# Expert stage: result stores on ScalarE's queue, and a landing tile with a GpSimd copy for the gathered rows

## The chip, the core and the metric

The kernel runs on one core of a Trainium2 chip. Its time is the device time of one execution, in microseconds; lower is better. TensorE multiplies, VectorE, ScalarE and GpSimd work on tiles, SyncE only issues DMAs. All five engines run their own instruction streams and wait for each other on semaphores.

## What is computed

The reference is a transformer block with attention, gated linear attention and a mixture of experts, followed by a second block. Only the mixture of experts matters here. 512 tokens choose 4 of 32 experts each. Cut to the core:

```python
top_v, top_i = lax.top_k(logits, TOP_K)                 # T=512 tokens, TOP_K=4, N_EXPERTS=32
gates = jax.nn.softmax(top_v, axis=-1)
...
def expert_block(args):
    idx, e = args
    xb = xpad[idx]                                      # the rows of this expert's tokens
    gu = xb @ w_gate_up[e] + b_gate_up[e]               # 1024 -> 2 x 1024
    x_glu = jnp.minimum(gu[:, ::2], SWIGLU_LIMIT)
    x_lin = jnp.clip(gu[:, 1::2], -SWIGLU_LIMIT, SWIGLU_LIMIT)
    act = x_glu * jax.nn.sigmoid(SWIGLU_ALPHA * x_glu) * (x_lin + 1.0)
    return act @ w_down[e] + b_down[e]                  # 1024 -> 1024
```

Everything is float32. Each expert has 12 MB of weights. The rows are then weighted with the gates and summed per token, which is done in a later stage.

## The kernel before

The expert stage is `stage_experts`, line 1536 on. Tokens are grouped by expert into units of 32 slots. An expert has as many units as its tokens need, at least one, so the number of units is known only at run time; each engine reads it from a table and loops over the units (`Fori(1, units)`), with the first unit written out ahead of the loop.

A row of 1024 numbers is laid out as four quarters of 256: the 128 partitions of the tile `rows` are 4 quarters x 32 slots. For a unit, TensorE does the following, in this order: the up part (L1727: eight slabs, each times a piece of the transposed rows), the down part of the unit before (L1750: four slabs), the transposes of the hidden values (L1736), the transposes of the rows of the next unit but one (`turn_rows`, L1704), and the bias (L1714).

Weights come as slabs of 1 MB, twelve per expert (8 up, 4 down). SyncE loads them in order, once per expert (L1653), into 18 slots of `staging`; a slot is free when the last unit of its expert has used it (`free`, L1627 on), and SyncE waits for the slab loaded four before (`arrived`, L1637). A quarter of each slab is used where it lies. The other three quarters are copied into a `ring` of four places, by VectorE (L1853, eight slabs of a unit) or ScalarE (L1785, four).

The rows of a unit come by an indirect DMA that GpSimd issues. `gather(i)` reads the unit's code from the table, waits until the last gather has landed and until TensorE has transposed the rows that lie in `rows` (semaphore `rows_ps`), copies the slot numbers (L1673), and issues the DMA (L1676) into `rows`. Gather 0 goes into the tile `y`, which is not in use yet.

The result of a unit is read from PSUM into the one tile `y` by ScalarE (`read_y`, L1808), which waits for the semaphore `y_free`. `store_rows` on GpSimd waits for that read, issues the store to `expert_rows` in HBM (L1683), waits until it has landed, and gives `y` back. The order on GpSimd inside the loop is

```python
with pool.Fori(1, units) as i:
    gather(i + 2)
    store_rows(i)
```

so the next gather is issued behind the landing of the store. The last result is stored by SyncE (L1660). On ScalarE the order in the loop is: ring copies, `gate` (L1791), `rows_turned` (L1802), a ring copy, `read_y`, `hidden_turned` (L1796).

Of the kernel before, what the change touches and what calls it, by code (L numbers as in the profile page):

```python
# [21 lines left out]
P = 128  # L22
S = 512
NT = S // P
D = 1024
# [7 lines left out]
NE, TOPK = 32, 4  # L33
# [1502 lines left out]
def stage_experts(k):  # L1536

    nc, d = k.nc, k.d
    with ExitStack() as ctx:
# [5 lines left out]
        quarter = sb("quarter", [P, P])  # L1545
        pick = sb("pick", [P, P], F32R)
        slot = sb("slot", [P, LINE], I32)
        rows = sb("rows", [P, D // QUARTERS])
        rowsT = sb("rowsT", [P, 2, P])
        lin = sb("lin", [P, GLU])  # L1550
# [14 lines left out]
        slot_ready = sem("slot_ready")  # L1565
        slot_seen = sem("slot_seen")
        rows_in = sem("rows_in")
        rows_ps = sem("rows_ps")
        rowsT_ready = sem("rowsT_ready")
        chunk_in = sem("chunk_in")  # L1570
# [6 lines left out]
        turned_ps = sem("hidden_turned_ps")  # L1577
        hT_ready = sem("hiddenT_ready")
        y_read = sem("expert_y_read")
        y_out = sem("expert_y_out")  # L1580
        y_free = sem("expert_y_free")
        last_out = sem("expert_last_out")
        settled = sem("early_settled")
        gate_diff = sem("gate_diff")
        gate_exp = sem("gate_exp")
# [32 lines left out]
        def store_of(n):  # L1618
            return d["expert_rows"][bass.ds(n, SLOTS), :].rearrange("r (c n) -> c r n", c=QUARTERS)

        with nc.Block() as block:
            @block.sync
            def _(sp):
                up = lambda e, q: d["w_gate_up"][(e * KT + q) * P:(e * KT + q + 1) * P, :]
                down = lambda e, m: d["w_down"][(e * 4 + m) * P:(e * 4 + m + 1) * P, :]

                def free(c, last):  # L1627

                    if c < KT:
                        sp.wait_ge(chunk_done, last * CHUNKS + (c + 1))  # L1630
                    else:
                        sp.wait_ge(chunk_done, last * CHUNKS + (CHUNKS + c + 1))

                def arrived(m):

                    sp.wait_ge(raw_in[m % STAGED], 16 * (m // STAGED + 1))
                    sp.sem_inc(chunk_in, 1)  # L1637

                for c in range(QUARTERS):
                    sp.dma_start(raw_bias[c * NE:(c + 1) * NE, :], d["b_gate_up"][:, c * PART:(c + 1) * PART]  # L1640
                                 ).then_inc(bias_in, 16)
                sp.dma_start(quarter[:], d["quarters"]).then_inc(quarter_in, 16)
                for m in range(EARLY - AHEAD):
                    arrived(m)
                for m in range(EARLY, NE * CHUNKS):
                    e, c = m // CHUNKS, m % CHUNKS
                    old = m - STAGED
                    if old >= 0:
                        if old % CHUNKS == 0 or old == 0:
                            of = old // CHUNKS  # L1650
                            last = sp.value_load(k.table[0:1, ENDS + of:ENDS + of + 1], min_val=0, max_val=NBLK - 1)
                        free(old % CHUNKS, last)
                    sp.dma_start(staging[:, m % STAGED * CHUNK:(m % STAGED + 1) * CHUNK],  # L1653
                                 up(e, c) if c < KT else down(e, c - KT)).then_inc(raw_in[m % STAGED], 16)
                    arrived(m - AHEAD)
                for m in range(NE * CHUNKS - AHEAD, NE * CHUNKS):
                    arrived(m)
                end = sp.value_load(k.table[0:1, TABLE - 2:TABLE - 1], min_val=NE - 1, max_val=NBLK - 1)
                sp.wait_ge(y_read, end + 1)
                sp.dma_start(store_of(end * SLOTS), y[:]).then_inc(last_out, 16)  # L1660
                sp.wait_ge(last_out, 16)

            @block.gpsimd
            def _(pool):
                units = units_on(pool)
                by_quarter = d["h2"].rearrange("t (c n) -> (t c) n", c=QUARTERS)

                def gather(i, out=rows, at=0):
                    code = pool.value_load(k.table[0:1, bass.ds(i + P, 1)], min_val=0, max_val=CODES - 1)
                    if out is rows:  # L1670
                        after(pool, rows_in, 16 * i)
                        after(pool, rows_ps, i)
                    pool.tensor_copy(slot[:, at:at + 1], k.slots[:, bass.ds(code, 1)]).then_inc(slot_ready, 1)  # L1673
                    pool.wait_ge(slot_ready, i + 1)
                    pool.sem_inc(slot_seen, 1)
                    pool.indirect_dma_start(  # L1676
                        out=out[:], out_offset=None, in_=by_quarter,
                        in_offset=bass.IndirectOffsetOnAxis(ap=slot[:, at:at + 1], axis=0)).then_inc(rows_in, 16)

                def store_rows(n):  # L1680

                    pool.wait_ge(y_read, n)
                    pool.dma_start(store_of(n * SLOTS - SLOTS), y[:]).then_inc(y_out, 16)  # L1683
                    pool.wait_ge(y_out, 16 * n)
                    pool.sem_inc(y_free, 1)

                gather(0, y, 1)
                gather(1)
                gather(2)
                with pool.Fori(1, units) as i:  # L1690
                    gather(i + 2)
                    store_rows(i)
                pool.wait_ge(rows_in, 16 * units + 32)

            @block.tensor
            def _(pe):
# [1 line left out]
                ident = k.sq[:, IDENT, :]  # L1698

                def turn_rows(i, src=rows):  # L1700
                    pe.wait_ge(rows_in, 16 * i + 16)
                    after(pe, rowsT_ready, i)
                    for b in range(2):
                        mm = pe.transpose(k.bank(6)[:, b * P:(b + 1) * P], src[:, b * P:(b + 1) * P], ident)  # L1704
                    mm.then_inc(rows_ps, 1)
# [73 lines left out]
            def _(act):  # L1779
# [24 lines left out]

                def read_y(n, done):
                    act.wait_ge(chunk_done, done)
                    act.wait_ge(y_free, n + 1)
                    act.activation(y[:], k.bank(4)[:, 0:GLU], ACT.Copy).then_inc(y_read, 1)  # L1808

                act.sem_inc(y_free, 1)  # L1810
                rows_turned(0, 0)
                fill(0, 0, 2)
                act.wait_ge(bias_set, 1)
# [13 lines left out]
                with act.Fori(1, units) as i:  # L1827
                    e = expert_on(act, i)
                    fill(i, e, 5)
                    fill(i, e, 7)  # L1830
                    fill(i, expert_on(act, i - 1), 10)
                    gate(i)
                    rows_turned(i + 1, i * CHUNKS + KT)
                    fill(i + 1, expert_on(act, i + 1), 2)
                    read_y(i - 1, i * CHUNKS + CHUNKS)
                    hidden_turned(i)
                act.wait_ge(act_filled, units * len(BY_ACT) + 1)
                act.sem_inc(act_filled, 2)
# [2 lines left out]
                act.activation(k.gates[:], k.gates[:], ACT.Exp).then_inc(gate_exp, 1)  # L1841
                end = act.value_load(k.table[0:1, TABLE - 2:TABLE - 1], min_val=NE - 1, max_val=NBLK - 1)
                read_y(end, units * CHUNKS + CHUNKS)

            @block.vector
            def _(dve):
# [1273 lines left out]
```

## Time and profile before

| | |
|---|---|
| Median of 3 runs | 2101.05 us (2095.19 to 2104.95) |
| The profiled execution | 2098.68 us |
| Its span in the profile | 2097.1 us |
| TensorE busy | 1704.3 us, 81% |
| VectorE busy | 1136.5 us |
| ScalarE busy | 853.6 us |
| GpSimd busy | 257.8 us |
| Mean granted TensorE clock | 0.897 of full speed |
| DMA | 516.46 MB, mean 246 GB/s |

The profile is one execution. The page of the profile lists each engine's busy time, the span in 40 slices, and the costliest groups of instructions; the trace behind it gives single instructions with their start, the idle time of their engine ahead of them and what ended it. The expert stage is the stretch from about 376 to 1694 us. A granted clock of 1.00 is 2.4 GHz, 0.50 is 1.2 GHz.

### The profile page before, as it was taken

The numbers are of one execution on the slowest core, as the hardware profiler recorded it, in microseconds if no ns is written. First come the engines' busy times: TensorE is split into PE (matmuls) and PEld (weight loads), VectorE is DVE, ScalarE is ACT, GpSimd is POOL, SyncE is SP. The second block draws the span as 40 slices with busy tenths as digits, with TensorE's granted clock in tenths as the row PEclk, the third lists the DMA queues.
The fourth block names the chain that finished last, engine by engine and source line by source line (L and its number), as shares of the span: only waits on it lengthen the run. The fifth ranks groups of instructions, "written<-read, shape, count | busy, mean of one in ns | idle before, by whom it ended". The sixth has DMA issues, their size and how long they took to land. (4 is left out here: it accounts for less than half of the span.)

```text
span 2097.1 us, 50062 instructions
## 1 busy us (share of the span) xinstructions
PE 1704.3 (81%) x16925; PEld 894.4 (43%) x16926; DVE 1136.5 (54%) x1698; ACT 853.6 (41%) x1131; POOL 257.8 (12%) x304
## 2 busy tenths in 40 slices
PE   6999898677977787878887787879778657999797
PEld 4999644232332332323332233323323125777763
DVE  5874536554654554545654555546545356694555
ACT  5344521543543443434543444434444234442421
POOL 0000000211111111111111111111111030151000
PEclk9999998897998888989987889889988777999999
DMA  8871840659478866995389985997598983231011
GB/s 301 277 242 33 216 190 21 260 220 423 163 305 335 336 265 259 394 381 221 137 343 404 424 337 222 371 400 302 205 415 344 417 308 80 73 91 42 4 52 40
DMA packets 135287, 516.46 MB, mean 246 GB/s; under 512 B 19927, under 2 KB 58728, under 8 KB 85929
## 3 DMA queue, kind: packets, MB, share of 16 engines
q1 hardware_dynamic: 117016, 483.74, 58.9%
q0 software_dynamic: 18048, 31.20, 4.5%
q8 instruction: 51, 0.84, 0.2%
q10 hardware_dynamic: 146, 0.48, 0.1%
q14 instruction: 26, 0.21, 0.0%
HBM read 492.44 MB, written 22.81 MB: 246 GB/s over the span
## 5 line engine op out<-in xcount | busy, mean ns | idle before, releaser
L1853 DVE COPY ring<-staging 128x1536 f32 (+1 forms) x638 | 600.5, 967 | 578.0 <-PE banks L1727 464.3
L1785 ACT ACTIVATE ring<-staging 128x1536 f32 (+1 forms) x319 | 473.8, 1487 | 731.6 <-PE banks L1727 545.9
L1727 PE MATMUL banks<-staging,rowsT 128*32 (+1 forms) x1268 | 633.5, 654 | 42.4 <-DVE ring L1853 21.3
L1727 PE MATMUL banks<-ring,rowsT 128*32 128x512 f32 x3840 | 641.9, 655 | 0.0
L1727 PEld LDWEIGHTS banks<-staging,rowsT 128*32 128x32 f32 x1268 | 140.8, 118 | 480.8 <-issue 476.6
L1750 PE MATMUL banks<-staging,hiddenT 128*32 x1280 | 294.0, 383 | 1.6 <-DVE ring L1853 1.3
L1750 PE MATMUL banks<-ring,hiddenT 128*32 128x256 f32 x3840 | 294.8, 383 | 0.0
L1704 PE MATMUL banks<-sq,rows 128*128 128x128 f32 x162 | 41.1, 343 | 234.5 <-DMA rows<-h_rows,slot 234.5
L1750 PEld LDWEIGHTS banks<-staging,hiddenT 128*32 128x32 f32 x1280 | 141.7, 111 | 153.7 <-issue 47.3
L1750 PEld LDWEIGHTS banks<-ring,hiddenT 128*32 128x32 f32 x3840 | 155.3, 111 | 0.0
L1727 PEld LDWEIGHTS banks<-ring,rowsT 128*32 128x32 f32 x3840 | 155.2, 118 | 0.0
L602 PE MATMUL banks<-w_in_hi,hT 128*128 128x256 f32 (+1 forms) x768 | 147.3, 291 | 1.5 <-issue 1.5
L1673 POOL COPY slot<-slots 128x1 int32 x82 | 30.2, 368 | 878.5 <-issue 857.8
L2196 PE MATMUL banks<-h3T,w_in_hi 128*128 128x512 f32 x400 | 129.4, 405 | 1.4 <-DVE h3T L2374 1.4
L1704 PEld LDWEIGHTS banks<-sq,rows 128*128 128x128 f32 x162 | 21.0, 165 | 245.1 <-DMA rows<-h_rows,slot 245.1
L602 PEld LDWEIGHTS banks<-w_in_hi,hT 128*128 128x128 f32 x768 | 122.5, 194 | 3.5 <-issue 3.5
L1683 POOL DMA_DIRECT2D expert_rows<-y_rows x79 | 62.8, 795 | 388.6 <-ACT y_rows L1808 365.7
L602 PE MATMUL banks<-w_in_lo,hT 128*128 128x256 f32 (+1 forms) x384 | 109.7, 286 | 0.0
L1676 POOL DMA_INDIRECT rows<-h_rows,slot x81 | 96.4, 1190 | 66.6 <-POOL slot L1673 51.0
L2196 PEld LDWEIGHTS banks<-h3T,w_in_hi 128*128 128x128 f32 x400 | 76.1, 191 | 23.1 <-issue 4.1
L2196 PE MATMUL banks<-h3T,w_in_lo 128*128 128x512 f32 x200 | 78.9, 395 | 0.0
L602 PEld LDWEIGHTS banks<-w_in_lo,hT 128*128 128x128 f32 x384 | 74.5, 194 | 1.9 <-issue 1.9
(434 smaller groups left out, 1939.2 us busy)
## 6 DMA issues: line engine op xcount, KB each, us to landing
staging<-in_w_gate_up SPq DMA_DIRECT2D x250, 1024.0 KB, 11.5
staging<-in_w_down SPq DMA_DIRECT2D x128, 1024.0 KB, 12.8
stage<-in_w_mod SPq DMA_DIRECT2D x21, 1024.0 KB, 5.8
stage<-in_w_in SPq DMA_DIRECT2D x25, 512.0 KB, 4.0
stage<-in_w_in SPq DMA_DIRECT2D x11, 1024.0 KB, 6.1
expert_rows<-y_rows POOLq DMA_DIRECT2D x79, 128.0 KB, 8.6
expert_rows<-catT SPq DMA_DIRECT2D x1, 7936.0 KB
early<-in_w_gate_up SPq DMA_DIRECT2D x6, 1024.0 KB, 12.9
```

What stands on the lines that cost most here:

```text
L602: mm = pe.matmul(k.bank(4 + t)[:, 0:w], hT[:, a, q, tt], b[:, q, :], start=(q == 0 and a == 0 and b is hi), stop=(q == KT - 1 and a == 1))
L1673: pool.tensor_copy(slot[:, at:at + 1], k.slots[:, bass.ds(code, 1)]).then_inc(slot_ready, 1)
L1676: pool.indirect_dma_start(out=out[:], out_offset=None, in_=by_quarter, in_offset=bass.IndirectOffsetOnAxis(ap=slot[:, at:at + 1], axis=0)) ...
L1683: pool.dma_start(store_of(n * SLOTS - SLOTS), y[:]).then_inc(y_out, 16)
L1704: mm = pe.transpose(k.bank(6)[:, b * P:(b + 1) * P], src[:, b * P:(b + 1) * P], ident)
L1727: mm = pe.matmul(k.bank(0)[c * SLOTS:(c + 1) * SLOTS, :], rowsT[:, q % 2, row], w, start=first and q == 0, stop=not first and q == KT - 1, ...
L1750: mm = pe.matmul(k.bank(4)[c * SLOTS:(c + 1) * SLOTS, 0:GLU], hT[:, b, m * SLOTS:(m + 1) * SLOTS], w, start=(m == 0 and b == 0), stop=(m = ...
L1785: act.activation(ring[:, pos % RING, :], staged(i, e, pos, PART, CHUNK - PART), ACT.Copy).then_inc(act_filled, 1)
L1853: dve.tensor_copy(ring[:, pos % RING, :], staged(i, e, pos, PART, CHUNK - PART)).then_inc(dve_filled, 1)
L2196: mm = pe.matmul(k.bank(n % 4), w[:, n % NW, q, :], hT[:, b, q, :], start=(q == 0 and a == 0), stop=(q == KT - 1 and a == 2))
```

## The change

- The result rows are stored by ScalarE's DMA queue: `store_y` follows `read_y` on ScalarE, and waits for ScalarE's own copy. `read_y` waits for the landing of the store before (semaphore `y_out`); `y_free` and `last_out` are gone, as is SyncE's final store.
- A new tile `landing`, as large as `rows`. From the third on, all gathers go into it. GpSimd copies `landing` to `rows` (`move_rows`) when TensorE has transposed what lay in `rows`, and then issues the next gather. So the loop on GpSimd is `move_rows(i + 2)`, `gather(i + 3)`. The first three gathers go to three tiles and wait for nothing of each other.
- TensorE's `turn_rows` waits for the semaphore `rows_here`, that the GpSimd copy sets, in place of the gather's own.

```diff
@@ SyncE
-                end = sp.value_load(k.table[0:1, TABLE - 2:TABLE - 1], min_val=NE - 1, max_val=NBLK - 1)
-                sp.wait_ge(y_read, end + 1)
-                sp.dma_start(store_of(end * SLOTS), y[:]).then_inc(last_out, 16)
-                sp.wait_ge(last_out, 16)
@@ GpSimd
-                def gather(i, out=rows, at=0):
+                def gather(i, out, at, done):
                     code = pool.value_load(k.table[0:1, bass.ds(i + P, 1)], min_val=0, max_val=CODES - 1)
-                    if out is rows:
-                        after(pool, rows_in, 16 * i)
-                        after(pool, rows_ps, i)
                     pool.tensor_copy(slot[:, at:at + 1], k.slots[:, bass.ds(code, 1)]).then_inc(slot_ready, 1)
...
-                def store_rows(n):
-
-                    pool.wait_ge(y_read, n)
-                    pool.dma_start(store_of(n * SLOTS - SLOTS), y[:]).then_inc(y_out, 16)
-                    pool.wait_ge(y_out, 16 * n)
-                    pool.sem_inc(y_free, 1)
-
-                gather(0, y, 1)
-                gather(1)
-                gather(2)
+                def move_rows(i):
+                    pool.wait_ge(rows_in, 16 * i - 16)
+                    pool.wait_ge(rows_ps, i)
+                    pool.sem_inc(rows_free, 1)
+                    pool.tensor_copy(rows[:], landing[:]).then_inc(rows_here, 1)
+                    pool.wait_ge(rows_here, i + 1)
+                    pool.sem_inc(rows_moved, 1)
+
+                gather(0, y, 1, first_in[0])
+                gather(1, rows, 2, first_in[1])
+                gather(2, landing, 0, rows_in)
+                for m in range(2):
+                    pool.wait_ge(first_in[m], 16)
+                    pool.sem_inc(rows_here, 1)
+                move_rows(2)
+                gather(3, landing, 0, rows_in)
                 with pool.Fori(1, units) as i:
-                    gather(i + 2)
-                    store_rows(i)
-                pool.wait_ge(rows_in, 16 * units + 32)
+                    move_rows(i + 2)
+                    gather(i + 3, landing, 0, rows_in)
+                pool.wait_ge(rows_in, 16 * units + 16)
@@ TensorE
                 def turn_rows(i, src=rows):
-                    pe.wait_ge(rows_in, 16 * i + 16)
+                    pe.wait_ge(rows_here, i + 1)
@@ ScalarE
                 def read_y(n, done):
                     act.wait_ge(chunk_done, done)
-                    act.wait_ge(y_free, n + 1)
+                    act.wait_ge(y_out, 16 * n + 16)
                     act.activation(y[:], k.bank(4)[:, 0:GLU], ACT.Copy).then_inc(y_read, 1)
 
-                act.sem_inc(y_free, 1)
+                def store_y(n):
+                    act.wait_ge(y_read, n + 1)
+                    act.sem_inc(y_seen, 1)
+                    act.dma_start(store_of(n * SLOTS), y[:]).then_inc(y_out, 16)
+
+                act.sem_inc(y_out, 16)
...
                     read_y(i - 1, i * CHUNKS + CHUNKS)
+                    store_y(i - 1)
                     hidden_turned(i)
...
                 read_y(end, units * CHUNKS + CHUNKS)
+                store_y(end)
+                act.wait_ge(y_out, 16 * units + 16)
+                act.sem_inc(y_seen, 1)
```

## Rows read from the trace of the kernel before

**Rows 1.** TensorE's waits, 370 to 1700 us: in total, times, longest (us).
```profile
PE banks L1704 <- DMA rows<-h_rows,slot: 234.5, 41, 9.6
PE banks L1727 <- DVE ring L1853: 21.3, 18, 6.0
PE banks L1727 <- ACT ring L1785: 14.1, 11, 1.9
```

**Rows 2.** Timeline of TensorE's L1704 and GpSimd: start, us, what, [idle before <-releaser].
```profile
914.17 0.38 PE L1704 MATMUL banks<-sq,rows 128*128 128x128 f32 x2
933.77 0.69 PE L1704 MATMUL banks<-sq,rows 128*128 128x128 f32 x2 [7.78 <-DMA rows<-h_rows,slot]
948.37 0.38 PE L1704 MATMUL banks<-sq,rows 128*128 128x128 f32 x2
...
915.86 0.76 POOL L1683 DMA_DIRECT2D expert_rows<-y_rows  x1 [9.28 <-ACT y_rows L1808]
925.60 0.75 POOL L1673 COPY slot<-slots 128x1 int32 x1 [8.98 <-issue]
927.18 0.99 POOL L1676 DMA_INDIRECT rows<-h_rows,slot  x1 [0.82 <-ACT y_rows L1808]
```

**Rows 3.** Issue to landing by line: first the stores L1683, then the gathers L1676.
```profile
DMA to landing us min/median/max: 3.7/8.6/9.9
...
DMA to landing us min/median/max: 2.7/6.1/7.9
```

**Rows 4.** Timeline of TensorE's L1704 where no weights are being loaded.
```profile
1005.03 0.38 PE L1704 MATMUL banks<-sq,rows 128*128 128x128 f32 x2
...
1029.35 0.38 PE L1704 MATMUL banks<-sq,rows 128*128 128x128 f32 x2
```

**Rows 5.** Stretches: PE, PEld, DVE, ACT, POOL busy, PEclk, DMA share, GB/s.
```profile
1005.00:1029.00 24.00, 23.00 (x268) 9.37 (x266) 16.51 (x23) 13.76 (x17) 5.06 (x6) 1.00 0.08 22
1140.00:1180.00 40.00, 28.25 (x256) 9.88 (x256) 16.96 (x22) 14.15 (x17) 4.90 (x7) 0.73 1.01 424
484.00:492.00 8.00, 6.85 (x78) 2.91 (x75) 3.63 (x6) 3.92 (x5) 1.09 (x2) 0.66 1.01 427
```

**Rows 6.** SyncE's waits for free slots, 370 to 1700 us: total, times, longest.
```profile
SPq L1653 <- PE banks L1727: 420.5, 104, 68.7
...
SPq L1653 <- PE banks L1750: 250.2, 107, 16.1
```

**Rows 7.** Issue to landing of the weight slabs, L1653, 370 to 1700 us.
```profile
DMA to landing us min/median/max: 4.7/12.1/15.1
```

**Rows 8.** Timeline of TensorE in a unit of an expert with one unit.
```profile
482.19 1.06 PE L1727 MATMUL banks<-staging,rowsT 128*32 x1 [1.14 <-DVE ring L1853]
...
485.28 1.05 PE L1727 MATMUL banks<-staging,rowsT 128*32 x1 [1.15 <-ACT ring L1785]
```

**Rows 9.** Timeline of ScalarE, behind a result read and at the kernel's start.
```profile
949.25 0.38 ACT L1796 ACTIVATE hiddenT<-banks 128x256 f32<-128x256 f32 x1
951.36 1.49 ACT L1785 ACTIVATE ring<-staging 128x1536 f32 x1 [1.73 <-PE banks L1727]
...
0.92 0.41 ACTq L422 DMA_DIRECT2D sq<-in_square  x1
```

**Rows 10.** First and last turn of the loop, and L1808: min/median/max ns, first and last start.
```profile
395.50 0.38 PE L1704 MATMUL banks<-sq,rows 128*128 128x128 f32 x2
...
1687.54 0.44 PE L1704 MATMUL banks<-sq,rows 128*128 128x128 f32 x2 [0.41 <-DMA rows<-h_rows,slot]
...
L1808 ACT ACTIVATE y_rows<-banks x80: 362/366/384, 409.9 to 1693.7; 128x256 f32<-128x256 f32 x80
```

**Rows 11.** A GpSimd copy (busy, mean ns), all ring copies L1853, and one of them.
```profile
L2320 POOL COPY sums<-z 128x512 f32<-128x512 f32 x4 | 2.9, 719 | 104.3 <-ACT z L2258 104.1
...
L1853 DVE COPY ring<-staging x638: 940/960/1196, 387.4 to 1690.7; 128x1536 f32 x158, 128x1536 f32<-128x1536 f32 x2
...
950.46 1.12 DVE L1853 COPY ring<-staging 128x1536 f32 x1 [0.69 <-PE banks L1727]
```

More of the change, by code:

```diff
@@ L1547, in stage_experts @@
         slot = sb("slot", [P, LINE], I32)
+        landing = sb("rows_landing", [P, D // QUARTERS])
         rows = sb("rows", [P, D // QUARTERS])
@@ L1567, in stage_experts @@
         rows_in = sem("rows_in")
+        first_in = [sem(f"first_rows{m}_in") for m in range(2)]
+        rows_here = sem("rows_here")
+        rows_free = sem("rows_free")
+        rows_moved = sem("rows_moved")
         rows_ps = sem("rows_ps")
@@ L1579, in stage_experts @@
         y_read = sem("expert_y_read")
+        y_seen = sem("expert_y_seen")
         y_out = sem("expert_y_out")
-        y_free = sem("expert_y_free")
-        last_out = sem("expert_last_out")
         settled = sem("early_settled")
@@ L1677, in gather @@
                         out=out[:], out_offset=None, in_=by_quarter,
-                        in_offset=bass.IndirectOffsetOnAxis(ap=slot[:, at:at + 1], axis=0)).then_inc(rows_in, 16)
-                def store_rows(n):
-                    pool.wait_ge(y_read, n)
-                    pool.dma_start(store_of(n * SLOTS - SLOTS), y[:]).then_inc(y_out, 16)
-                    pool.wait_ge(y_out, 16 * n)
-                    pool.sem_inc(y_free, 1)
-                gather(0, y, 1)
-                gather(1)
-                gather(2)
+                        in_offset=bass.IndirectOffsetOnAxis(ap=slot[:, at:at + 1], axis=0)).then_inc(done, 16)
+                def move_rows(i):
[13 more added lines that the diff above has]
+                gather(3, landing, 0, rows_in)
                 with pool.Fori(1, units) as i:
-                    gather(i + 2)
-                    store_rows(i)
-                pool.wait_ge(rows_in, 16 * units + 32)
+                    move_rows(i + 2)
+                    gather(i + 3, landing, 0, rows_in)
+                pool.wait_ge(rows_in, 16 * units + 16)
             @block.tensor
```

## Prediction, made before the change was run

> **What bounds the kernel now.** I read the page first for where TensorE is busy, then TensorE's waits in the expert stage, then the stretch of one unit on TensorE and GpSimd, then SyncE's waits and the DMA rates, because a wait that goes will show what is behind it. The loop of the expert stage, 79 units on TensorE, runs from the row transposes at 395.5 us to those at 1687.5 us [rows 10], so 1292 of 2097 us; the last result is read at 1693.7. In the stage TensorE waits for almost one thing: 234.5 us, in 41 waits, for the gathered rows in front of the transposes of L1704, against 21.3 and 14.1 us for weight copies into the ring [rows 1]. The weights are not late today because this wait gives them time.
>
> The wait comes from one tile and one queue. GpSimd issues the store of unit n's result, waits until it has landed, and only then copies the next slot numbers and issues the next gather. In the stretch of [rows 2] TensorE turned rows at 914.17, the store went out at 915.86, the slot copy ran at 925.60, the gather was issued at 927.18, and TensorE went on at 933.77 after 7.78 us idle: 17.9 us from store to rows. Store and gather take a median of 8.6 and 6.1 us to land [rows 3]. The next turn, at 948.37, was 14.6 us later without a wait. So a pair costs 948.37 - 914.17 = 34.2 us, 17.1 us per unit. Where no weights are on the way (22 GB/s), two units take 1029.35 - 1005.03 = 24.3 us [rows 4, 5]: 12.1 us per unit, at a granted clock of 1.00. The average of the loop is 1292 / 79 = 16.35.
>
> **What the change removes.** It takes the 8-us store landing off GpSimd and gives the gather a tile of its own. After turn n on TensorE, GpSimd copies rows n+1 over and issues the gather n+2: copy with its waits under 2 us, slot copy to issue 1.6 us (925.60 to 927.18, [rows 2]), landing at most 7.9 us [rows 3]: about 11.5 us after the turn. Those rows are needed by the second turn after, at least 24 us on. So I take the rows wait to zero: 234.5 us, and 2.5 us of the first gathers, which no longer wait for each other. After each such wait TensorE also ran slow: turn to turn it took 14.6 us here, against 12.1. Over the loop this is what is left: 1292 - 79 x 12.1 - 234.5 - 36 = 66 us. If nothing else came late, the loop would be 79 x 12.1 = 956 us.
>
> **What is late next: the weights.** This is the term that decides. Each expert's weights are loaded once, 12 slabs of 1.049 MB, however many units of 32 slots it has. With the DMA engines saturated the traffic is 424 GB/s at a share of 1.01 [rows 5], so a slab takes 2.47 us, an expert's twelve 29.6 us, and the gather and store of one unit (262 KB) 0.6 us. An expert with n units gives TensorE 12.1 n us of work. So n = 1 falls 18.1 us short, n = 2 falls 6.6 us short, n = 3 gains 4.9. SyncE says the same of today's schedule: it waits 420.5 + 250.2 = 671 us for free slots, up to 68.7 us at once [rows 6]. The loading is idle behind long experts and cannot be ahead by more than the ring of 18 slots.
>
> How many units each expert has follows from the reference's router on its own inputs: 5 1 2 5 3 2 2 3 3 3 2 2 2 7 2 2 1 2 2 3 4 2 2 2 3 4 1 2 3 1 1 1, 80 in all, as many as L1808 has instructions [rows 10]. The lead behind a long expert I work out so. I take it that at the start of its last unit the ring holds the next expert's first six slabs. The first slot is free 0.9 us later, the first slab lands 4.7 us after its issue (shortest landing, [rows 7]), one more takes 2.5, its ring copy 1.1: 9.2 us. TensorE comes to the last up-slab of the expert behind it after 12.1 + 6.0 us. The difference less 0.6 us of the unit's own traffic is 8.3 us. Then run by run: experts 1-2: 18.1 + 6.6 - 8.3 = 16.4; 5-6: 4.9; 10-12: 11.5; 14-18: 36.2; 21-23: 11.5; 26-27: 16.4; 29-30, with only the 4.9 gained by expert 28 before them: 31.3. Sum 128 us of waiting for weights, against 36 today. Such a unit is to be seen now: from 482.19 to 485.28 us one slab's matmuls follow the other's at 3.1 us, with a wait of 1.15 us for the ring before each [rows 8], and in 484 to 492 the granted clock is 0.66 [rows 5]. TensorE's next four slabs, already there, then ran at the lower level for some 2.5 us, 1.3 us dearer. Seven runs to all 15 waiting units: 9 to 20, I take 12.
>
> **What it adds.** ScalarE: behind each result read it now waits for its own copy (0.37 us), then issues a DMA. Its DMA issue at the kernel's start took 0.41 us [rows 9]; with address arithmetic I allow 0.7 us. That pushes hiddenT (949.25) by 0.7 us, which TensorE needs 7 us later, behind the whole up part, and the next ring copy at 951.36 has 1.73 us of idle in front of it [rows 9]. Cost nothing; if that cover were gone, 0.7 x 80 = 56 us. GpSimd: one copy of 128x256 per unit. No such copy is in the trace; one of 128x512 took 719 ns [rows 11], so between 0.36 and 0.72; I take 0.5. On GpSimd itself it is free. Against VectorE it may cost: a ring copy that began at 950.46, while GpSimd issued its store, took 1.12 us instead of 0.96 [rows 11]. That store issue leaves GpSimd, the copy comes. Bounds: from a gain of 79 x 0.16 = 13 us to a loss of 79 x 0.5 = 40 us if each copy stood before a ring copy that TensorE waits for. Most ring copies have over 1 us of slack, so 5. ScalarE's read of the next result now waits for its queue's own store; it has 11 us for the 8.6 of today's [rows 3]: nothing, and rival (d) otherwise. The final store, SyncE's so far, is one DMA from another queue: nothing.
>
> The Trainium skill, on its page "SBUF — State Buffer", section "Who interferes with whom", speaks against this part: VectorE in its two-port copy mode and GpSimd share a port pair as an exclusive lock, and whichever comes second blocks for the whole instruction. The 1.12 us row agrees in kind, as a partial overlap would. By that rule alone the term would be the 40 us just named.
>
> **The sum.** The turn that closes unit 0 is at 395.5 now [rows 10] and 2.5 us earlier then: 393.0. 79 units x 12.1 = 955.9. Weights 128. Restart at the slow clock 12. Lock 5. That gives 1494 for the last turn, at 1687.5 now [rows 10]. The last expert's four down-slabs come some 3 us late: 1497. So the gain is 190 us. The profiled execution took 2098.7 us, so 1908.7; the median of the runs shown is 2.4 us above it, 2101.05, so 1911.
>
> **The rivals.**
> (a) The lock decides: the GpSimd copy delays a ring copy on TensorE's path in most units. For it: the 1.12 us row, and the copy comes right at the unit's edge, when VectorE fills the next unit's first slabs. Against it: VectorE's ring copies have a maximum of 1.20 us over 638 today, though GpSimd works beside them. 35 us more: 1946.
> (b) The lead is worth nothing, since gathers and stores also break into the slab stream: seven runs x 8.3 us = 58 us more: 1969.
> (c) The lead is worth more, a whole six slabs (15 us): five runs save 6.5 us, and run 5-6 the 4.9: some 37 us less: 1874.
> (d) The other side: ScalarE's store lands behind the slabs. SyncE's slabs take 12.1 us to land in the median and 15.1 at most [rows 7]. ScalarE's next read waits for its last store, so a unit can't be shorter than the landing and 0.9 us. Below 11 us this is free, and the idle 1.73 us of ScalarE take it to some 13; at the slabs' 15.1 in every unit the loop is 79 x 16 = 1264 us, 2073, and from 15.5 on (16.35 - 0.9) the change is slower than before: 17 us would give 79 x 17.9 = 1414 us, 2223. Against it: GpSimd's store landed in 8.6 us among the same slabs.
> (e) It doesn't do what it says: a copy or a semaphore in GpSimd's chain keeps rows late. The chain of 11.5 us would have to double. Then 2100.
>
> **How the numbers follow.** My forecast, with its terms off by up to 20 us either way, 0.62: 1890 to 1931. (a) 0.12, (b) 0.09, (c) 0.08, (d) 0.06, of which 0.03 slower than before and the rest between 2000 and 2090, (e) 0.03. The range reaches to (c) and (b), 1872 to 1972; outside lie (d), (e) and tails. 0.5% is 10 us, about what a measurement of this kernel can tell from no change. Faster: all but (e) and a half of (d): 0.94. Same 0.03, slower 0.03.
>
> **What would show it.** TensorE's waits at L1704 for the gathered rows, 234.5 us, should be under 10, and no wait for the GpSimd copy should stand in their place. TensorE's waits for VectorE's and ScalarE's ring copies should rise from 36 to between 90 and 150 us, in the units of the runs named, above all the last three experts and experts 14 to 18. Units elsewhere should repeat at 12.1 us. The DMA rate over the loop should rise by a sixth (1292 / 1101). ScalarE's store should land in under 12 us. VectorE's ring copies should stay near 0.97 us in the mean; 1.1 or more would be (a). I am wrong if rows waits remain, or if weight waits sum to over 200 us.

## The result: half the forecast gain

| | before | changed |
|---|---|---|
| Median | 2098.12 us (4 runs) | 1999.86 us (4 runs, 1998.11 to 2001.35) |
| Ratio | | 0.9528, 95% interval 0.9499 to 0.9556 |
| Profiled execution | 2098.68 us | 1999.55 us |
| Span | 2097.1 us | 1997.8 us |
| Loop of 79 units, first to last turn of rows | 395.5 to 1687.5: 1292 us | 395.9 to 1589.5: 1194 us |

The change is 98 us faster, where 190 was forecast; the time lies above the range of 1872 to 1972. All of the difference is in the loop. The last row is from the timeline of TensorE, where these two lines are the turns that [rows 10] has for before:

```profile
395.85 0.63 PE L1707 MATMUL banks<-sq,rows 128*128 128x128 f32 x2
...
1589.54 0.38 PE L1707 MATMUL banks<-sq,rows 128*128 128x128 f32 x2
```

The view of waits, 370 to 1600 us, says what TensorE waits for now (total, times, longest), and the last line what ScalarE does:

```profile
PE banks L1730 <- ACT ring L1788: 149.8, 92, 4.7
PE banks L1730 <- DVE ring L1865: 33.6, 32, 5.4
...
ACT y_rows L1811 <- DMA expert_rows<-y_rows: 97.5, 36, 4.5
```

The wait for rows in L1704, 234.5 us in [rows 1], is gone altogether: L1707 has none left but that for the very first gather. The new wait is for ring copies, as forecast, but nearly all of it for ScalarE's (14.1 us before), and ScalarE itself waits 97.5 us for its own stores. That is the wait that rival (d) named. ScalarE's timeline in one unit (start, us, what, idle before and its releaser) shows its size:

```profile
900.60 0.39 ACT L1811 ACTIVATE y_rows<-banks 128x256 f32<-128x256 f32 x1 [1.63 <-DMA expert_rows<-y_rows]
901.25 1.07 ACTq L1816 DMA_DIRECT2D expert_rows<-y_rows  x1
902.42 0.38 ACT L1799 ACTIVATE hiddenT<-banks 128x256 f32<-128x256 f32 x1 [1.44 <-PE banks L1730]
903.85 2.86 ACT L1788 ACTIVATE ring<-staging 128x1536 f32 x2 [1.04 <-PE banks L1730]
...
916.62 0.38 ACT L1811 ACTIVATE y_rows<-banks 128x256 f32<-128x256 f32 x1 [4.01 <-DMA expert_rows<-y_rows]
```

The store is issued at 901.25, and the next read starts at 916.62, after 4.01 us of waiting for it: 15.4 us of landing, where GpSimd's stores had a median of 8.6 and a maximum of 9.9 [rows 3]. The issue holds ScalarE for 1.07 us (0.41 in [rows 9]), and hiddenT comes 1.82 us after the start of the read; before, the two started 0.26 us apart.

### The profile page after: what moved, and what is told of

Same layout as the page of the kernel before. It is cut to its first block and busy times, and to the rows that moved or that the text cites. A ratio compares the mean times of both kernels' runs of the same rounds, so it can differ in the third digit from the quotient of the medians.

```text
span 1997.8 us, 50227 instructions
## 1 busy us (share of the span) xinstructions
PE 1695.5 (85%) x16925; PEld 877.7 (44%) x16926; DVE 1139.1 (57%) x1698; ACT 859.4 (43%) x1131; POOL 326.4 (16%) x307
## 5 line engine op out<-in xcount | busy, mean ns | idle before, releaser
L1730 PE MATMUL banks<-staging,rowsT 128*32 (+1 forms) x1268 | 650.1, 654 | 185.0 <-ACT ring L1788 149.8
L1730 PE MATMUL banks<-ring,rowsT 128*32 128x512 f32 x3840 | 661.1, 656 | 0.0
L1730 PEld LDWEIGHTS banks<-staging,rowsT 128*32 128x32 f32 x1268 | 128.8, 115 | 630.3 <-issue 625.4
L1681 POOL COPY rows<-rows_landing 128x256 f32<-128x256 f32 x80 | 74.8, 935 | 794.9 <-PE banks L1707 794.9
L1730 PEld LDWEIGHTS banks<-ring,rowsT 128*32 128x32 f32 x3840 | 144.9, 115 | 0.0
L1673 POOL DMA_INDIRECT rows_landing<-h_rows,slot x81 | 133.4, 1647 | 64.3 <-POOL slot L1670 64.3
L1670 POOL COPY slot<-slots 128x1 int32 x83 | 49.4, 595 | 276.0 <-issue 206.2
L1874 DVE TENSOR_SCALAR lin<-banks 128x256 f32<-128x256 f32 x80 | 34.0, 425 | 96.3 <-PE banks L1730 96.3
L1799 ACT ACTIVATE hiddenT<-banks 128x256 f32<-128x256 f32 x80 | 30.7, 384 | 113.0 <-PE banks L1730 98.7
L1811 ACT ACTIVATE y_rows<-banks 128x256 f32<-128x256 f32 x80 | 30.0, 375 | 108.3 <-DMA expert_rows<-y_rows 97.5
## 6 DMA issues: line engine op xcount, KB each, us to landing
staging<-in_w_gate_up SPq DMA_DIRECT2D x250, 1024.0 KB, 13.3
staging<-in_w_down SPq DMA_DIRECT2D x128, 1024.0 KB, 13.3
```

The lines of the kernel that those rows point to most:

```text
L1673: pool.indirect_dma_start(out=out[:], out_offset=None, in_=by_quarter, in_offset=bass.IndirectOffsetOnAxis(ap=slot[:, at:at + 1], axis=0)) ...
L1681: pool.tensor_copy(rows[:], landing[:]).then_inc(rows_here, 1)
L1730: mm = pe.matmul(k.bank(0)[c * SLOTS:(c + 1) * SLOTS, :], rowsT[:, q % 2, row], w, start=first and q == 0, stop=not first and q == KT - 1, ...
L1799: act.activation(hT[:].rearrange("p b n -> p (b n)"), k.bank(2)[:, 0:2 * P], ACT.Copy, scale=1.0 / ALPHA).then_inc(hT_ready, 1)
L1874: dve.tensor_scalar(lin[:], k.bank(0)[:, GLU:PART], LIMIT + 1.0, 1.0 - LIMIT, ALU.min, ALU.max).then_inc(lin_ready, 1)
```

## Experiments

The theories: **A**, ScalarE waits for the landing of its own store; **B**, the issue of the store on ScalarE makes its ring copies late; **C**, the GpSimd copy locks VectorE out; **D**, the weights are later than the ledger has them (the ledger is the prediction's count of slab time against unit time, expert by expert); later **E**, ScalarE's stores slow the weights. All loops below are from the first to the last turn of rows of the profiled execution, as above. The diffs are cut to the lines that matter.

| Kernel | median, us | ratio to before | loop, us |
|---|---|---|---|
| changed | 1999.9 | 0.953 (0.950 to 0.956) | 1194 |
| ScalarE's stores, no landing wait | 1948.8 | 0.931 (0.928 to 0.934) | 1141 |
| the same, issue moved | 1932.8 | 0.923 (0.914 to 0.932) | 1130 |
| the same, no stores in the loop | | | 1069 |
| GpSimd's stores, landing tile | 1902.9 | 0.909 (0.9065 to 0.9114) | 1096 |
| GpSimd's stores, wait moved only | 1933.2 | 0.923 (0.9211 to 0.9250) | 1127 |
| ScalarE's stores only | 1991.7 | 0.951 (0.948 to 0.955) | 1182 |

A ratio is to the kernel before in the same set of runs; in the five sets that kernel's medians lie between 2089.7 and 2098.1 us, so a few microseconds between two rows' medians mean nothing. A loop is of one execution; for two versions that differ only in GpSimd's copies it is 1095.8 and 1095.9. The versions without the landing wait, with the issue moved and with no stores in the loop leave the results out: what they store is an unchanged tile. The last stores it behind the loop, in one execution, so only its loop is compared.

### Take ScalarE's wait for the landing away

The result is read into another tile, so that no DMA has to have landed; the stores go on, without the results.

```diff
                 def read_y(n, done):
                     act.wait_ge(chunk_done, done)
-                    act.wait_ge(y_out, 16 * n + 16)
-                    act.activation(y[:], k.bank(4)[:, 0:GLU], ACT.Copy).then_inc(y_read, 1)
+                    act.activation(y_kept[:], k.bank(4)[:, 0:GLU], ACT.Copy).then_inc(y_read, 1)
```

> The changed kernel, with ScalarE reading each result into a tile of its own that no DMA touches, so that no result read waits for the landing of the store before. ScalarE still issues all 80 stores, which now send an unchanged tile: the stored rows are not the results. Theory A (landing: the store on ScalarE's queue lands about 15 us after its issue while slabs are on the way, against 8.6 from GpSimd; ScalarE waits for it and its ring copies come late): the loop falls from 1193 to 1100-1115 us, the time to 1908-1925, TensorE's waits for ScalarE's ring copies from 150 to 60 us or less. Theory B (issue: the 1.07 us that ScalarE spends on issuing a store, and the 1.4 us in front of hiddenT, use up its slack): stays at 1985-2000. Theory C (the GpSimd copy locks VectorE out) and theory D (weights are later than the ledger has them): stays at 1985-2000.

Measured: 1948.8 us, loop 1141, against 1908 to 1925 and 1100 to 1115 expected. A is true, and it is worth 51 us (53 of loop), not the 85 it was to explain. TensorE still waits 79.9 us for ScalarE's ring copies, 102 times, and 52.5 us for VectorE's:

```profile
PE banks L1731 <- ACT ring L1789: 79.9, 102, 2.3
PE banks L1731 <- DVE ring L1865: 52.5, 44, 4.4
```

### Give the stores back to GpSimd, keep the rest

```diff
                 with pool.Fori(1, units) as i:
                     move_rows(i + 2)
                     gather(i + 3, landing, 0, rows_in)
+                    pool.wait_ge(y_read, i)
+                    pool.sem_inc(y_seen, 1)
+                    pool.dma_start(store_of(i * SLOTS - SLOTS), y[:]).then_inc(y_out, 16)
...
                     read_y(i - 1, i * CHUNKS + CHUNKS)
-                    store_y(i - 1)
```

ScalarE still waits for `y_out` ahead of a read; GpSimd issues and goes on.

> The changed kernel, with the stores issued by GpSimd again, behind the gather in its loop, but without GpSimd waiting for their landing: ScalarE waits for it, as in the changed kernel. Landing tile and GpSimd copy stay. Theory A: the store lands in 8.6 us as in the kernel before, no wait of ScalarE is left, and the time is the one predicted for the change, 1905-1925. Theory B: the issue leaves ScalarE too, the same. Theories C and D: 1985-2000, since copy and weights are as in the changed kernel.

Measured: 1902.9 us (1897.3 to 1904.1), ratio 0.909. Of the versions that do all the work this is the fastest (a variant of it, below, is equal), 97 us faster than the changed kernel, and it is where the forecast put the change (1911). Copy and landing tile are in it, so C and D don't hold in that size. The lines are the turns that bound the loop and, between them, three turns in a row: 11.51 us for a unit with nothing late, then 22.24 us for one that waits for weights:

```profile
391.96 0.38 PE L1715 MATMUL banks<-sq,rows 128*128 128x128 f32 x2
...
1191.86 0.38 PE L1715 MATMUL banks<-sq,rows 128*128 128x128 f32 x2
1203.37 0.38 PE L1715 MATMUL banks<-sq,rows 128*128 128x128 f32 x2
1225.61 0.38 PE L1715 MATMUL banks<-sq,rows 128*128 128x128 f32 x2
...
1487.74 0.38 PE L1715 MATMUL banks<-sq,rows 128*128 128x128 f32 x2
```

### Fewer slabs under way

SyncE waits for the slab loaded two before, in place of four before.

```diff
-AHEAD = 4
+AHEAD = 2
```

> The changed kernel with SyncE waiting for the slab loaded two before instead of four before, so that about three slabs instead of five are under way when ScalarE issues a store. Theory A, with the store queued behind the slabs: it lands some 5 us sooner (10 us), ScalarE's waits for it (97 us) nearly go, and the time falls to 1915-1950 unless three slabs under way load more slowly. Theories B and C: no change, 1995-2005. Theory D: slower if anything.

Measured: 2005.7 us, ratio to before 0.958 (0.954 to 0.961), no gain over the changed kernel. The slabs' own landing fell from a median of 13.3 to 8.0 us (first line; the view of L1657), but the store's did not (the other two, ScalarE's timeline): issued at 843.95, still waited for until 858.53, 14.6 us.

```profile
DMA to landing us min/median/max: 4.7/8.0/10.1
...
843.95 1.07 ACTq L1816 DMA_DIRECT2D expert_rows<-y_rows  x1
858.53 0.38 ACT L1811 ACTIVATE y_rows<-banks 128x256 f32<-128x256 f32 x1 [1.51 <-DMA expert_rows<-y_rows]
```

So the picture in rival (d), a store queued behind the slabs, is wrong. What is left of it is the number.

### Halve the slabs' packets

Each slab is loaded by two DMAs of half its columns, so that a run in a partition is 4 KB.

```diff
-                    sp.dma_start(staging[:, m % STAGED * CHUNK:(m % STAGED + 1) * CHUNK],
-                                 up(e, c) if c < KT else down(e, c - KT)).then_inc(raw_in[m % STAGED], 16)
+                    for part in range(2):
+                        at, size = m % STAGED * CHUNK, CHUNK // 2
+                        sp.dma_start(staging[:, at + part * size:at + (part + 1) * size],
+                                     (up(e, c) if c < KT else down(e, c - KT))[:, part * size:(part + 1) * size]
+                                     ).then_inc(raw_in[m % STAGED], 16)
```

> The changed kernel, each 1 MB slab loaded by two DMAs of half its columns, so that a partition's run is 4 KB instead of 8 KB and the slabs' packets are half as long. In the changed kernel the packets of ScalarE's store are served from 3.9 to 14.3 us after its issue, and the same with two slabs fewer under way, so it doesn't wait behind the slabs but takes turns with them. If turns are taken packet by packet (A1), halved slab packets bring the store's last packet to 8-10 us, ScalarE's waits of 97 us for it nearly go, and the time falls to 1945-1965. If it is ScalarE's own issue of 1 KB rows that is slow (A2), the landing and the time stay: 1995-2005.

Measured: 1976.9 us, ratio to before 0.945 (0.943 to 0.947), the loop 1174: some 20 us faster than the changed kernel, where one theory had 35 or more and the other nothing. The mechanism of the first is there. The DMA view counts the packets of ScalarE's queue (q10; packets, MB, share). In the changed kernel, of the store issued at 901.25, 72 of its 132 packets are served in the first ten microseconds (901.3 to 911.3) and 60 after them (911.3 to 917):

```profile
q10 hardware_dynamic: 72, 0.07, 2.1%
...
q10 hardware_dynamic: 60, 0.06, 2.9%
```

With halved slab packets, of the store issued at 889.76, 128 in the first ten (889.7 to 899.7):

```profile
q10 hardware_dynamic: 128, 0.13, 3.7%
```

ScalarE's wait for its stores is gone. The store's 1 KB packets take turns with the slabs' packets, so what sets its landing is how long one turn of the other lasts, not how much of the other is queued. The Trainium skill, page "DMA: Bandwidth & Descriptors", section "Queues, rings and completion order", has it that a DMA engine goes round its queues packet by packet. The trace agrees: at the end of the store of 901.25, from 911.8 to 915.6, slab and store packets come in nearly equal numbers.

```profile
q1 hardware_dynamic: 45, 0.34, 20.9%
q10 hardware_dynamic: 48, 0.05, 3.6%
```

The shares say more: together 24.5% of 16 engines, so four are at work, and all of the store that is left is on them. Turns with 8 KB packets explain the 11 us only if the whole store is on these four, 32 packets on each: a slab packet takes 0.309 us in the trace and one of the store 0.046, and 32 turns of both are 11.4 us. From its first to its last packet the store took 11.1 us (905.2 to 916.3). The same sum holds in the other cases: with packets of 4 KB (0.159 us) 6.6 us, measured 6.3; with two slabs fewer under way 11.4 again, measured 10.8; where no slabs flow 1.5, measured 1.7.

For the weights halved packets are no gain (two take 0.318 us, one of 8 KB 0.309), and their waits at the ring stay, 85.7 and 65.3 us; for that part the expectation had too much.

### Move ScalarE's issue to where it is idle

In the version without the landing wait, the store's issue goes behind the pair of ring copies with which ScalarE's next turn of the loop begins. [rows 9] had 1.73 us of idle time behind hiddenT; that was the cover of this cost.

```diff
                     fill(i, e, 5)
                     fill(i, e, 7)
+                    act.dma_start(store_of(i * SLOTS - SLOTS), y[:]).then_inc(y_out, 16)
                     fill(i, expert_on(act, i - 1), 10)
...
                     read_y(i - 1, i * CHUNKS + CHUNKS)
-                    store_y(i - 1)
                     hidden_turned(i)
```

> The version without the landing wait (1949 us; it stores an unchanged tile), with ScalarE's store issue moved from behind the result read to behind the second ring copy of the next unit, where ScalarE waits about 1.1 us for TensorE anyway. Theory B (what is left of the loss, 1949 against 1903, is the place of the 1.07 us issue: it makes the ring copy of slab 5 0.4 us late in every unit): TensorE's tenth step of the up part starts 0.43 us after the one before instead of 0.8, a unit with nothing late takes 11.5 us instead of 11.9, and the time falls to 1903-1925. If the issue costs ScalarE this wherever it stands, or the rest is the store's own traffic on ScalarE's queue, it stays at 1940-1955.

Measured: 1932.8 us, 16 us faster (the intervals of the two ratios just meet), the loop 11 us shorter, and a unit with nothing late takes 11.51 us instead of 11.91, as B says. Where the 0.4 us sits is to be seen on TensorE in the changed kernel, at the tenth step of the up part, slab 5, which ScalarE copies; the pair of copies above it starts at 933.47:

```profile
933.47 2.86 ACT L1788 ACTIVATE ring<-staging 128x1536 f32 x2 [1.05 <-PE banks L1730]
...
934.30 0.59 PE L1730 MATMUL banks<-staging,rowsT 128*32 x1
935.10 0.61 PE L1730 MATMUL banks<-staging,rowsT 128*32 x1 [0.19 <-ACT ring L1788]
935.55 0.59 PE L1730 MATMUL banks<-staging,rowsT 128*32 x1
```

and in the version with GpSimd's stores, in the same unit, the steps follow at 0.43 us without a break, and ScalarE's two copies stand apart:

```profile
879.91 1.49 ACT L1796 ACTIVATE ring<-staging 128x1536 f32 x1 [1.74 <-PE banks L1738]
881.56 1.49 ACT L1796 ACTIVATE ring<-staging 128x1536 f32 x1 [0.16 <-PE banks L1738]
...
881.59 0.59 PE L1738 MATMUL banks<-staging,rowsT 128*32 x1
882.02 0.59 PE L1738 MATMUL banks<-staging,rowsT 128*32 x1
```

The time missed its expectation of 1903 to 1925. 58 units became 0.4 us shorter, 23 us, but the units that wait for weights got longer. 34 us of loop remain against the version with GpSimd's stores, all of them in such units (unit 31: 21.4 against 14.1 us).

### No stores in the loop at all

The version with the issue moved, its stores taken out of the loop and sent by SyncE behind the last slab.

```diff
+                sp.wait_ge(first_in[0], 16)
+                for n in range(NBLK):
+                    sp.dma_start(store_of(n * SLOTS), y[:]).then_inc(y_out, 16)
+                sp.wait_ge(y_out, 16 * NBLK)
...
-                    act.dma_start(store_of(i * SLOTS - SLOTS), y[:]).then_inc(y_out, 16)
...
-                store_y(end)
```

> The version with the store issue moved, now with no store in the loop at all; SyncE writes all 94 blocks of 32 rows from an unchanged tile behind the last slab instead, so only the loop (first to last turn of rows) is to be compared, not the time. With ScalarE's stores in it the loop takes 1130 us, with GpSimd's 1096. In the first, slabs land 13.4 us after their issue in the median, in the second 12.5. Theory E (stores on ScalarE's queue slow the stream of slabs, by more than their bytes): slabs land in 12.0-12.5 us and the loop takes 1075-1096 us. If the 34 us between the two have another cause on ScalarE or VectorE, only the stores' 10.5 MB go, at 424 GB/s 25 us less a part that is hidden: 1110-1130 us.

Measured: loop 1069 us, under the range of E (1075 to 1096). So the same 80 stores, of the same bytes, cost 1096 - 1069 = 27 us of loop from GpSimd's queue, and 1130 - 1069 = 61 us from ScalarE's. This run takes ScalarE's issue out of the loop together with the traffic, and the loop alone can't tell them apart; the stream of slabs can. Its landing is slower with ScalarE's stores than with none and with GpSimd's, in this order (in the first, the landing of only 60 or so slabs is known):

```profile
DMA to landing us min/median/max: 6.4/13.5/14.9
...
DMA to landing us min/median/max: 4.7/12.4/14.7
...
DMA to landing us min/median/max: 4.8/12.5/15.5
```

In seven stretches, 217 slabs in all, SyncE issues slab after slab, under 4 us apart, in all three versions. These take 540.3 us with no stores, 553.9 with GpSimd's (38 of them fall in) and 591.8 with ScalarE's (36). A store costs the slabs 0.36 us from GpSimd and 1.43 us from ScalarE, and the 38 us between the two are all of the 34 that are asked for. In the longest of the stretches, 60 slabs and ten stores, the columns are those of [rows 5]; again ScalarE's stores, none, GpSimd's:

```profile
954.20:1117.84 163.64, 130.37 (x1262) 43.47 (x1258) 79.75 (x105) 66.90 (x76) 22.88 (x30) 0.86 1.01 411
...
928.62:1078.60 149.98, 124.89 (x1256) 44.86 (x1260) 79.31 (x104) 66.87 (x77) 28.76 (x30) 0.90 1.01 427
...
935.83:1089.06 153.23, 124.97 (x1237) 44.21 (x1233) 78.66 (x103) 64.11 (x73) 31.12 (x38) 0.89 1.01 425
```

What sets the two queues apart is to be seen where no slabs flow. The DMA view of one store alone, ScalarE's in the changed kernel (930.9 to 935) and then GpSimd's (878.7 to 883.5):

```profile
DMA packets 132, 0.13 MB, mean 32 GB/s; under 512 B 4, under 2 KB 132, under 8 KB 132
...
DMA packets 144, 0.13 MB, mean 28 GB/s; under 512 B 112, under 2 KB 112, under 8 KB 144
```

From ScalarE the 128 KB go in 128 packets of 1 KB, with 4 of 4 bytes; from GpSimd in 32 packets of 4 KB, with 96 of 16 bytes and 16 of 4 bytes. Read together with the shares above: one 4-byte packet closes the DMA on each engine that it uses, four engines for ScalarE's store and all 16 for GpSimd's. ScalarE's store then takes 32 x 0.046 = 1.5 us of each of its four engines, and GpSimd's two packets of 0.159 us, 0.32 us, of each of 16. These are near the 1.43 and 0.36 us that a store costs the slabs, each of which has 16 closing packets and lands with the last of them. The agreement is close, but it is a reading of the traces: no run spread ScalarE's store over 16 engines. That the four come from the four quarters, the outermost dimension of `store_of`, is likely and not shown.

The Trainium skill, on the same page, section "Issuing engines are not separate DMA queues", has it that DMAs run on the same 16 DMA engines whichever engine started them, and that issuing from several engines saves only the time of the issue. The slabs' loss agrees with the shared engines. But here the issuing engine also changed how many of them the same store used, and in what packets.

### ScalarE's stores alone, and the moved wait alone

The kernel before, with the first part of the change only: stores and their landing wait on ScalarE, gathers as before.

```diff
                 with pool.Fori(1, units) as i:
                     gather(i + 2)
-                    store_rows(i)
...
-                    act.wait_ge(y_free, n + 1)
+                    act.wait_ge(y_out, 16 * n + 16)
...
                     read_y(i - 1, i * CHUNKS + CHUNKS)
+                    store_y(i - 1)
```

> The kernel before with the first part of the change alone: stores issued by ScalarE, gathers as before into the one tile of rows, with no landing tile and no GpSimd copy. All theories but C: with the store's landing off GpSimd, turn to rows takes 0.3 + 1.6 + 6 to 8 us, under the 12.1 of a unit, so the waits for rows go by this part alone, and the time is within 10 us of the changed kernel, 1990-2010. Theory C: without the copy it is faster, 1950 or less.

Measured: 1991.7 us, within the interval of the whole change; its loop is 12 us shorter. Beside ScalarE's stores the landing tile and the GpSimd copy bring nothing.

Then the kernel before with its stores left on GpSimd, which no longer waits for their landing:

```diff
                 def store_rows(n):
 
                     pool.wait_ge(y_read, n)
+                    pool.sem_inc(y_seen, 1)
                     pool.dma_start(store_of(n * SLOTS - SLOTS), y[:]).then_inc(y_out, 16)
-                    pool.wait_ge(y_out, 16 * n)
-                    pool.sem_inc(y_free, 1)
...
-                    act.wait_ge(y_free, n + 1)
+                    act.wait_ge(y_out, 16 * n + 16)
```

> The kernel before with one thing moved: GpSimd issues each store where it did but doesn't wait for its landing; ScalarE waits for it ahead of the next result read. No landing tile, no copy, no gather further ahead, nothing on ScalarE's queue. If the 8.6 us of landing on GpSimd were the whole of the wait for rows, and the landing tile and its copy buy nothing (A), this gives what the version with GpSimd's stores and the landing tile gave, 1895-1910: turn to rows takes 0.3 + 1.6 + 6.5 to 8 us, under the 11.5 of a unit. If the gather needs the second tile, waits for rows of 1 us or more per unit remain where slabs are under way, and the time is 1930 or more.

Measured: 1933.2 us. Moving one wait gives 160 of the 190 us to be had. The landing tile gives 30 more here, since the gather fits a unit only just: only 8 units take 11.51 us, and TensorE's waits still have rows among them:

```profile
PE banks L1732 <- ACT ring L1790: 53.8, 33, 2.7
PE banks L1732 <- DVE ring L1857: 47.8, 47, 4.2
PE banks L1709 <- DMA rows<-h_rows,slot: 25.5, 27, 2.7
PE banks L1732 <- issue: 11.9, 17, 0.8
```

### The price of the GpSimd copy

```diff
+                    pool.tensor_copy(spare_rows[:, 0:GLU // 2], landing[:, 0:GLU // 2])
+                    pool.tensor_copy(spare_rows[:, GLU // 2:], landing[:, GLU // 2:])
                     pool.tensor_copy(rows[:], landing[:]).then_inc(rows_here, 1)
```

> The version with GpSimd's stores and the landing tile, with GpSimd copying the landed rows a second time into a spare tile (two copies of 128x128), ahead of the copy that counts. Theory C (each GpSimd copy holds up a ring copy of VectorE on TensorE's path) gives 79 x 0.3 to 0.5 us more, 25-40: 1925-1945. The others: within 8 us of that version, 1895-1912.

Measured: 1901.9 us against 1902.9. The copy is free here; C falls. In these two versions, though, few copies meet a ring copy of VectorE (2 and 5 of the 80 that count). In the changed kernel 71 of 80 begin while one runs, and what is blocked is GpSimd: there its copies take from 397 to 1152 ns, with a median of 1091, while VectorE's ring copies have the median and the maximum that they had in [rows 11].

```profile
L1681 POOL COPY rows<-rows_landing x80: 397/1091/1152, 384.9 to 1557.5; 128x256 f32<-128x256 f32 x80
L1865 DVE COPY ring<-staging x638: 945/960/1187, 386.9 to 1591.2; 128x1536 f32 x158, 128x1536 f32<-128x1536 f32 x2
```

Each of the 71 ends 0.26 to 0.29 us after the ring copy that it met. This is the lock of the Trainium skill, page "SBUF — State Buffer", section "Who interferes with whom", where the second to issue is blocked until the first is done; the second was GpSimd nearly every time.

### The ledger of the weights

```diff
-                    sp.dma_start(staging[:, m % STAGED * CHUNK:(m % STAGED + 1) * CHUNK],
-                                 up(e, c) if c < KT else down(e, c - KT)).then_inc(raw_in[m % STAGED], 16)
+                    at, size = m % STAGED * CHUNK, CHUNK // 2 if m >= STAGED + EARLY else CHUNK
+                    sp.dma_start(staging[:, at:at + size],
+                                 (up(e, c) if c < KT else down(e, c - KT))[:, 0:size]).then_inc(raw_in[m % STAGED], 16)
```

> The version with GpSimd's stores and the landing tile, but from the 25th slab on only the first half of each weight slab is loaded (the other half of the slot keeps older weights, so the result is another one). Ledger of the weights: an expert's slabs then take 14.8 us instead of 29.6, and no expert but those with one unit is short, by about 4 us, less than the lead. The loop should be 79 x 11.5 us and a few more, 912-930 instead of 1096, and the time 1715-1740. If the loop's remaining 187 us over 79 x 11.5 had another cause than late weights, it stays above 1800.

Measured: 1746.9 us, and a loop of 935 us, from these turns, with TensorE's two waits for ring copies down to 16 us together:

```profile
396.40 0.38 PE L1716 MATMUL banks<-sq,rows 128*128 128x128 f32 x2
...
1331.84 0.38 PE L1716 MATMUL banks<-sq,rows 128*128 128x128 f32 x2
...
PE banks L1739 <- ACT ring L1797: 8.2, 12, 1.1
PE banks L1739 <- DVE ring L1864: 7.8, 8, 1.5
```

The loop is 5 us, the time 7 us over the ranges; in substance the ledger holds: of the 187 us that the loop has beyond 79 x 11.5, 160 are late weights.

## Why the prediction failed, step by step

**The bound and the stall.** Right. The wait for rows was the bound, it came from the store's landing on GpSimd, and it went to zero.

**A unit with nothing late, 12.1 us.** Too long: 11.51, in 59 of the 79 units of the version with GpSimd's stores, and 11.9 with ScalarE's. The pair of [rows 4] was not free of the stall. Its middle turn waited for the gather, and the rows so late put off the first slab behind it by 0.84 us more, 1.3 us in two units:

```profile
1017.00 0.44 PE L1704 MATMUL banks<-sq,rows 128*128 128x128 f32 x2 [0.30 <-DMA rows<-h_rows,slot]
```

This alone made the forecast 47 us too long.

**The weights, 128 us, and 12 of restarts.** Too small for such a short unit, and the pattern right. In the version with GpSimd's stores the units longer than 11.51 us are, but for the first, those of the seven runs named, and their excess is, run by run, 25.5, 12.9, 18.3, 47.2, 20.8, 24.7 and 34.7 us, 184 in all; forecast were 16.4, 4.9, 11.5, 36.2, 11.5, 16.4 and 31.3. With 11.5 us for a unit the same ledger gives 153 us of weights; what remains is some 4 us per run, where the restart was taken at 1.7; whether all of it is restart is not shown. For that version the sum came to 1494 for the last turn, and 1488 was measured: two errors, of 47 and of 41 us, that cancelled. That it lands so near the 1911 us of the forecast is in part luck.

**ScalarE's issue, nothing.** The failed step, first part. It was allowed 0.7 us against a cover of 1.73. It takes 1.07, with the waits around it puts hiddenT off by 1.6 us, and the ring copy that the cover stood in front of ends 0.4 us late. It is 0.4 us in each unit with nothing late; moving it is worth 11 us of loop. The fallback price of 0.7 x 80 us was an upper bound that held.

**ScalarE's read waits for its own store: 8.6 us in 11, nothing.** The failed step, main part. The landing was taken from GpSimd's queue, [rows 3], for a DMA on another one. It is 15.4 us while slabs flow, since on ScalarE's queue 32 packets on each of four DMA engines take turns with slab packets. Taking the wait away is worth 51 us. Rival (d) had the place, the threshold and nearly the landing (15.1), and the wrong reason, so it got a chance of 0.06; its 2073 us were for that landing in every unit, and ScalarE waited in 36 of them. The one row that spoke against it was of the wrong queue.

**The traffic of the stores, the same as before.** The failed step, third part, and in no rival: from ScalarE's queue a store costs the slabs 1.43 us, from GpSimd's 0.36. 34 us of loop.

The three add up: 1194 - 1141 = 53, 1141 - 1130 = 11 and 1130 - 1096 = 34 are the 98 us of loop between the changed kernel and the version with GpSimd's stores.

**The lock, 5 us.** It is nothing; rival (a) falls. Rivals (b) and (c) were about the lead that a long expert gives the weights. The ledger was off by tens of microseconds, but not by that: with GpSimd's stores it came to the forecast time, and the changed kernel missed it for the three reasons above.

## What to carry to other kernels

Moving a wait away from an engine and moving its DMA to another queue are two changes; do the first alone, and price the second by a DMA of that size on that queue beside the same traffic, for landing, issue and what it does to the traffic. The packets of such a DMA, and how many closing ones it has, show over how many DMA engines it goes. When a stall is taken out, count what each engine's next unit needs from DMA, unit by unit: here 12 slabs per expert against 1 to 7 units of work said where every remaining wait would be. A unit's length read beside a stall is not its length without one.

## What the runs showed of the hardware

- The same store of 128 KB went in 128 packets of 1 KB with 4 closing ones when ScalarE issued it, and in 32 packets of 4 KB with 16 closing ones (and 96 of 16 bytes) when GpSimd did. The shares fit 4 DMA engines for ScalarE's.
- Beside loads in 8 KB packets ScalarE's store lands after about 15 us; with two slabs fewer under way it is the same, with 4 KB packets of loads it is under 12. GpSimd's has a median of 9.1 us.
- 80 such stores lengthen a loop that is bound by 1 MB loads in part of its units by 27 us from GpSimd and by 61 us from ScalarE.
- A DMA issue with a computed address held ScalarE for 1.07 us, one with a fixed address, of another tile, for 0.41 us.
- GpSimd's 128x256 copy takes 0.40 to 1.15 us beside VectorE's ring copies, and left their median at 0.96 us and their maximum at 1.19.
